# Value products of a head pair moved behind the next pair's transposes, and a context layer that steps by whole heads

## What is computed

```python
# first block, per layer: 3 mixers x 8 heads
s = q @ k.T * scale + bias              # 256 x 256 per head, chunk-causal or causal
p = softmax(s)
y_h = p @ v_h                           # 64 wide per head
branches = stack([y_a, y_b, y_c]); proj = branches @ w_branch
merged = sum(sigmoid(x @ w_gate + b_gate) * proj) @ w_out

# second block, context layer: 8 heads, each with two score maps
p = softmax(q @ k.T / 8)                # q, k: 2 maps x 64 wide
a = p[:, 0] - lam * p[:, 1]
y_h = a @ v_h                           # 128 wide per head
```

## Time and profile before

| | us |
|---|---|
| median of 3 runs | 2656.06 (2655.84 to 2657.03) |
| the profiled execution | 2656.9 |
| its span, first to last instruction | 2655.1 |
| PE busy | 2633.1 (99%) |
| POOL busy | 1941.5 (73%) |
| ACT busy | 1419.6 (53%) |
| DVE busy | 1179.5 (44%) |

### The profile page before, as it was taken

How to read it: one execution, slowest core, us unless ns; L and a number is a source line. 1 busy time by engine, 2 the same in 40 slices (tenths; PEclk the granted TensorE clock), 3 DMA queues, 4 the chain that set the end, 5 groups by cost and what they waited for, 6 DMA issues and landing times.

```text
span 2655.1 us, 44218 instructions
## 1 busy us (share of the span) xinstructions
PE 2633.1 (99%) x17695; PEld 2292.0 (86%) x17695; DVE 1179.5 (44%) x2347; ACT 1419.6 (53%) x2002; POOL 1941.5 (73%) x816
## 2 busy tenths in 40 slices
PE   9999999999999999999999999999999999999999
PEld 8878889989878899888789998887899988878898
DVE  3443342234334433434435553545445544542655
ACT  5755554447565544455654446556544455564543
POOL 6657668856667488687677886866768877668787
PEclk9999999999999999999999999999999999999999
DMA  7556475565565655664454555644445565345453
GB/s 291 204 217 230 157 248 185 188 231 191 212 231 192 230 189 185 198 213 160 156 175 161 189 190 184 204 149 137 158 153 196 185 220 178 129 135 177 165 191 127
DMA packets 139085, 498.43 MB, mean 188 GB/s; under 512 B 15488, under 2 KB 17664, under 8 KB 137984
## 3 DMA queue, kind: packets, MB, share of 16 engines
q1 hardware_dynamic: 132768, 480.52, 53.6%
q10 hardware_dynamic: 6112, 15.08, 1.7%
HBM read 492.39 MB, written 3.15 MB: 187 GB/s over the span
## 4 chain that ended last, share of the span: by engine, by line
PE 94%; DVE 2%; ACT 1%; DVEq 1%; issue 0%; ACTq 0%; DMA 0%; SPq 0%; POOL 0%
PE lin L796 13%; PE lin L614 12%; PE lin L664 11%; PE lin L665 11%; PE lin L668 11%; PE aux L610 5%; PE aux L614 5%; PE aux L611 5%; PE lin L610 5%; PE lin L611 5%; PE aux L1183 2%; PE aux L1201 1%; PE aux L874 1%; PE aux L842 1%; PE lin L842 1%; PE aux L1190 1%
## 5 line engine op out<-in xcount | busy, mean ns | idle before, releaser
L576 POOL TENSOR_TENSOR wlo<-raw,whi 128x1024 fp32r<-128x1024 f32 x812 | 1941.3, 2407 | 703.4 <-ACT whi L1300 695.4
L1300 ACT ACTIVATE whi<-raw 128x1024 fp32r<-128x1024 f32 x811 | 845.3, 1057 | 649.6 <-PE lin L668 259.7
L796 PE MATMUL lin<-in_both,whi 128*128 128x512 f32 x1600 | 401.6, 393 | 0.2
L664 PE MATMUL lin<-whi,in_both 128*128 128x512 f32 x942 | 378.8, 402 | 0.3 <-DVE mods_all L1824 0.3
L665 PE MATMUL lin<-whi,in_both 128*128 128x512 f32 x942 | 368.1, 391 | 0.0
L614 PE MATMUL lin<-in_both,wlo 128*128 128x256 f32 x2560 | 365.7, 283 | 0.1
L614 PEld LDWEIGHTS lin<-in_both,wlo 128*128 128x128 f32 x2560 | 346.1, 192 | 16.1 <-POOL wlo L576 0.5
L796 PEld LDWEIGHTS lin<-in_both,whi 128*128 128x128 f32 x1600 | 287.7, 189 | 53.1 <-DVEq L2287 0.8
L2272 DVE TENSOR_REDUCE Z<-lin 128x512 f32<-128x1024 f32 x100 | 122.4, 1224 | 298.4 <-PE lin L614 297.0
L668 PE MATMUL lin<-wlo,in_both 128*128 128x512 f32 x944 | 253.6, 390 | 0.0
L610 PE MATMUL lin<-in_both,whi 128*128 128x256 f32 x920 | 234.6, 291 | 6.8 <-ACT whi L1762 6.4
(11 more groups left out here) (293 smaller groups left out, 3682.7 us busy)
## 6 DMA issues: line engine op xcount, KB each, us to landing
raw<-in_wstream SPq DMA_DIRECT2D x907, 512.0 KB, 3.5
gate_row<-in_gate_bias ACTq DMA_DIRECT2D x12, 256.0 KB, 3.3
Z<-in_rel ACTq DMA_DIRECT2D x2, 1536.0 KB, 11.5
Z<-in_mem_t ACTq DMA_DIRECT2D x2, 1024.0 KB, 7.2
kv_store<-Z ACTq DMA_DIRECT2D x2, 1024.0 KB, 8.9
Z<-kv_store ACTq DMA_DIRECT2D x2, 1024.0 KB, 9.9
Z<-in_ctx_t SPq DMA_DIRECT2D x1, 1024.0 KB, 7.3
out_x<-x SPq DMA_DIRECT2D x4, 256.0 KB, 2.5
```

The lines of the kernel that those rows point to most:

```text
L576: pool.tensor_tensor(wlo[s][:, :], raw[i % RAWS][:, :], whi[s][:, :].bitcast(F32), ALU.subtract).then_inc(lo_pool, 1)
L664: pe.matmul(out, xh, wh, start=start, stop=False, skip_group_check=True)
L796: pe.matmul(lin[:, p, up * CH:(up + 1) * CH], wh[:, w], in_both[:, :, k * T:(k + 1) * T], start=(k == 0), stop=(k == KD - 1), skip_group_c ...
L1300: act.activation(whi[s % SLOTS][:, :], raw[i % RAWS][:, :], ACT.Copy).then_inc(hi_ready, 1)
```

## The change

**First block.** `pair_values(p - 1)` now stands between `pair_transposes(p)` and `pair_scores(p + 1)`, so the fill of a pair is one stretch; only the last pair keeps its value products between fill. The products are written into columns 384 to 511 of banks 2 and 3 (`pair_output`), which makes six matmuls of 128 columns out of two of 256 and two of 128. The modulation tiles of both heads of a pair add up in bank 0, so DVE adds one row tile per pair instead of two. ACT takes `pair_hi(p - 1)` at the head of the pair and waits for `y_lo_done` before it copies the transposed probabilities; DVE takes `pair_lo(p - 1)` at the head of the pair, before `lowest`. The transposed modulation columns go to bank 1, and PE waits for `mod_added` ahead of the scores of the seventh pair.

**Context layer.** Where `kts == 2`, the 16 half-head steps become 8 head steps (`head_scores`, `head_transposes`, `head_outputs`, `head_exps`, `head_highest`, `head_combine`). The matmuls are the same ones; fill goes in blocks of 3 units before the values and 1 or 2 before the transposes, 36 units as before.

```diff
+HEAD_BEFORE_T = [1, 2] * (NH // 2)
+HEAD_BEFORE_V = [3] * NH
...
+        pair_output = aux[:, 2:4, SW:CH]
+        mod_out = aux[:, 1, SW:SW + 2 * TURN]
...
                 for g in heads:
-                    modulation_tile(aux[:, g % 2, SW:CH], g % TURN, True, True)
+                    modulation_tile(aux[:, 0, SW:CH], g % TURN, g == heads[0], g == heads[1])
+                if p and 2 * p % TURN == 0:
+                    pe.wait_ge(mod_added, t.ahead(mod_added, 2 * p // TURN))
...
+                for tt in range(2):
+                    for e in range(2):
+                        pe.matmul(aux[64 * e:64 * e + 64, 2 + tt, SW:CH], v[:, (h + e) * 64:(h + e + 1) * 64],
+                                  probs_tr(e)[:, tt * P:(tt + 1) * P], start=True, stop=(tt == 0), skip_group_check=True)
                 for e in range(2):
-                    pe.matmul(aux[64 * e:64 * e + 64, 2, 0:T], v[:, (h + e) * 64:(h + e + 1) * 64], probs_tr(e)[:, 0:T],
...
@@ PE, first_layer
                     pair_transposes(p)
+                    if p:
+                        pair_values(p - 1)
                     if p + 1 < PAIRS:
                         pair_scores(p + 1)
                     advance(fill, BEFORE_PV[p])
-                    pair_values(p)
+                    if p + 1 == PAIRS:
+                        pe.wait_ge(pt_ready, t.next(pt_ready, 2))
+                        pair_values(p)
                     advance(fill, AFTER_PV[p])
...
@@ ACT, first_layer
                 for p in range(PAIRS):
+                    if p:
+                        pair_hi(p - 1)
+                        act.wait_ge(y_lo_done, t.next(y_lo_done))
                     for e in range(2):
                         transposed(SW, e)
...
@@ DVE, first_layer
                 for p in range(PAIRS):
+                    if p:
+                        pair_lo(p - 1)
+                    if (2 * p + 2) % TURN == 0:
+                        modulation_bias(l, 2 * p + 2 - TURN, mod_out, TURN).then_inc(mod_added, 1)
...
@@ PE, second_layer
-                for n in range(STEPS):
+                if kts == 2:
+                    for h in range(NH):
+                        advance(fill, HEAD_BEFORE_T[h])
+                        head_transposes(h)
+                        if h + 1 < NH:
+                            head_scores(h + 1)
+                        advance(fill, HEAD_BEFORE_V[h])
+                        head_outputs(h)
```

More of the change, by code:

```diff
@@ L1205, in diff_values, with head_scores, head_transposes, head_outputs @@
                     t.skip(yb_taken)
+            def head_scores(h):
+                for tt in range(2):
+                    for m in range(2):
+                        q = zt(Q2 + h)[64 * m:64 * m + 64, tt * P:(tt + 1) * P]
+                        mm = pe.matmul(aux[:, m, tt * T:(tt + 1) * T], q, head_keys(m, h, 2), start=True, stop=True)
+                mm.then_inc(scores_done, 1)
+            def head_transposes(h):
+                pe.wait_ge(probs_ready, t.next(probs_ready))
+                for i in range(4):
+                    c = h % 2 * CH + i * P
+                    mm = pe.transpose(aux[:, 2, i * P:(i + 1) * P], probs[:, c:c + P], ident)
+                mm.then_inc(trans_done, 1)
+            def head_outputs(h):
+                if t.ahead(yb_taken, 0):
+                    pe.wait_ge(yb_taken, t.ahead(yb_taken, 0))
+                if h == 0:
+                    pe.wait_ge(values_ready, t.next(values_ready))
+                pe.wait_ge(pt_ready, t.next(pt_ready))
+                for tt in range(2):
+                    for kt in range(2):
+                        i = 2 * tt + kt
+                        mm = pe.matmul(aux[:, 3, tt * P:(tt + 1) * P], probs_tr(0)[:, i * P:(i + 1) * P], head_values(h, kt, 2),
+                                       start=(kt == 0), stop=(kt == 1))
+                    mm.then_inc(pv_done, 1)
+                t.skip(yb_taken)
             def second_fill():
@@ L1249, in second_layer @@
                 fill = second_fill()
-                for n in range(STEPS):
+                if kts == 2:
+                    for h in range(NH):
[5 more added lines that the diff above has]
+                        head_outputs(h)
+                for n in range(STEPS if kts == 4 else 0):
                     advance(fill, DIFF_BEFORE_T[n])
@@ L1660, in diff_exps, with head_exps @@
                 act.drain().then_inc(exp_done, 1)
+            def head_exps(h):
+                act.wait_ge(maxed, t.next(maxed))
+                for tt in range(2):
+                    for m in range(2):
+                        s = aux[:, m, tt * T:(tt + 1) * T]
+                        i = slice(2 * tt + m, 2 * tt + m + 1)
+                        act.activation(s, s, ACT.Exp, bias=stat(h, "minus", 4)[:, i], accum_out=stat(h, "total", 4)[:, i])
+                act.drain().then_inc(exp_done, 1)
             def gates_out(p, dst):
@@ L1729, in second_layer @@
                 fill = second_fill()
-                for n in range(STEPS):
+                if kts == 2:
+                    for h in range(NH):
+                        advance(fill, HEAD_BEFORE_T[h])
+                        transposed(CH)
+                        if h + 1 < NH:
+                            head_exps(h + 1)
+                        advance(fill, HEAD_BEFORE_V[h])
+                for n in range(STEPS if kts == 4 else 0):
                     advance(fill, DIFF_BEFORE_T[n])
@@ L1952, in lowest @@
                                              accum_out=stat(g, "minus")[:, tt:tt + 1])
[L1953 to L1956, removed]
+                if g % 2 == 0:
+                    rows, new = mod_rows(g), aux[:, 0, SW:CH]
+                    i = copy(rows, new) if g % TURN == 0 else tt_(rows, rows, new, ALU.add)
+                    if (g + 2) % TURN == 0:
+                        i.then_inc(mod_row, 1)
                 settle().then_inc(maxed, 1)
```

80 lines of the change are left out of this document (61 added, 19 removed).

## The result

The changed kernel takes 2661.62 us (median of 22 runs, 2659.43 to 2663.21), the kernel before 2656.71 in the same comparison (22 runs, 2655.38 to 2659.13). The ratio is 1.0017, with a 95% interval of 1.0011 to 1.0024: 4.9 us slower, within the 0.2% that I had called no change, and 0.6 us above the upper end of my range. The forecast was 2657.0. It stood on a median of three runs, 2656.06; with 22 runs the kernel before is at 2656.71, so the difference was forecast at +1.0 and measured at +4.9.

A forecast was written before the change was run, and what follows sets the result against it. PE, busy 99% of the span, was taken to bound the kernel. First block +4.9 and context layer -3.9 gave +1.0 on the 2656.06 us median: forecast 2657.0, range 2648 to 2661.

The forecast's parts named there:

- The interruption: First block, PE: a value step costing 1.01 us in the fill costs 0.75 to 0.80 behind transposes, 0.24 saved.
- The chain of the second and third pair: First block: ACT and DVE run late, so PE waits some 2.7 us per layer before its fourth feature chunk.
- Rival A: First block: the third pair's delay hides and does not reach PE; 2648.6 us, chance 0.20.
- Rival C: First block: the value step is not cheaper behind transposes, +3.8, 2660.8 us; chance 0.07.
- rival B: The clock falls in the new wait, 1.7 us per layer: 2660.4 us, far end 2663; chance 0.18.
- The sixth pair's wait: First block: PE's scores wait for DVE's `mod_added` behind the forget tiles, 0.8 us per layer.
- The eleventh pair's values: First block: these products still follow the twelfth pair's transposes, where before they were done: +0.75 us per layer.
- The context layer: Whole-head steps save 0.40 us a head, -3.2 for eight, plus -0.7 for two waits: -3.9.
- the old waits: Context layer: PE's two waits, for ACT's copy behind a gate and for DVE, would go, worth -0.7 us.

The follow-up runs named there:

- the busy short wait: The change plus 11 bf16 matmuls of zeros in PE's wait before the fourth feature chunk: 2659.33 us, ratio 1.0007 to the kernel before.
- the long one: The change with ACT's third-pair probability copies done three times and 18 matmuls on zeros in each lengthened wait: 2663.97 us, ratio 1.0022 to the kernel before.
- the first block's part alone: First block as changed, context layer in half-head steps as in the kernel before: 2664.19 us, ratio 1.0028 to the kernel before.
- The longer bare wait: The change with ACT's third-pair probability copies done three times, PE left idle in the wait: 2667.61 us, ratio 1.0037 to the kernel before.
- the new context table: The change with value steps 1, 2, 3, 5 kept in the fill, later forget tiles and another context fill table: 2648.56 us, ratio 0.9967 to the kernel before.

## Why the prediction was wrong

**The interruption, 1.01 to 0.75 or 0.80:** right. It is 0.80, the dear end, and yet an interval is 0.22 to 0.28 shorter, around the 0.24 taken.

**The chain of the second and third pair:** right in each step. ACT goes on at 99.79 (forecast 99.9), PE starts its next feature chunk at 105.68 (105.9), the wait is 2.6 (2.7), PE is 2.6 behind at the fourth pair (2.8). Ahead of it PE waits near 72 and 84, 1.1 and 1.0 from start to start, and the third pair's transposes come at 94.05 instead of 93.55: the forecast's "nothing is gained, everything is 0.5 late". Rival A is out. It is the second pair's value step that bites there: keeping that one step in the fill gives back 2.2 of the 2.6. Rival C is out too, as the value step measured 0.80.

**The step that failed first: the clock behind the wait.** It was rival B, with a chance of 0.18, and I forecast a granted clock of 1.00 from 103 to 112. It is 0.50 in one of the two layers of both profiles of the change, and the sum held nothing for it. The forecast's difference was 3.9 short (+1.0 against +4.9); of that the stretches leave 2.1 to the clock, the busy short wait says 2.3, the long one 2.4, and the first block's part alone only 0.8. What I set against B (dense fill around the pause, and waits of about 1 us that left the clock alone) said nothing about 2.6, as no wait of that length was in the trace; a case that no row speaks against should have had more weight. The price was near: 1.7 each forecast, 1.4 and 1.5 measured, but not in every layer and execution. The Trainium skill (TensorE: Matmul & The Clock Gate, section HAM oscillation) describes a kernel in which waits of about 3 to 5 us between dense bursts put the array back to half its clock each time. The longer bare wait agrees (0.50 behind it in both layers of its profile). The forecast wait of 2.7 is shorter than those, so B did not follow from that page; behind the measured 2.6 the clock fell in two of six profiled waits.

**The wait behind the forget keys, 0.5 a layer, missing from the sum.** I asked of each moved step whom its own results make late, and not what it had covered. ACT's evacuation of 1.02 ran beside the fifth pair's values and the forget keys together; with the values gone the keys' 0.67 are too short. The rows of before near 134 show both side by side.

**The sixth pair's wait:** forecast 0.8, measured 0.7 (0.91 from start to start, where 0.2 is normal). Right.

**The eleventh pair's values:** +0.75 forecast, and from the twelfth pair's transposes to the merged output it is +0.9.

**The context layer, -3.9, or -3.2 if the waits come back:** -3.2. A head step's parts are 0.52 for the transposes and 1.07 for the scores, as forecast:

```profile
1284.38 0.60 PE L1228 MATMUL aux<-c,probs 128*128 128x128 f32 x4
1284.90 1.13 PE L1221 MATMUL aux<-Z 64*128 64x256 f32 x8
1285.97 0.50 PE L667 MATMUL lin<-whi,in_both 128*128 128x512 f32 x1
```

But the same fewer and larger steps that let the old waits go put four times 0.44 of DVE's work in one piece ahead of a tap that PE waits for.

**The sum.** Forecast +1.0. Forget keys +1.0, context layer +0.7, the chain at the fourth pair -0.4, the clock +2.3: +4.6, against a measured +4.9 and +4.5. That the two are so near is in part luck: without the clock these terms give +2.3 and the stretches +2.8, and the clock's 2.3 is the least certain of them. The direction and most terms were right. The range took B without its far end and held no term for a cover that is taken away. How far it was missed says little: on the 2656.06 that the forecast stood on, +4.9 is 2661.0, just at its upper end.

## What to carry to other kernels

When a step leaves a stretch of an engine, look at what ran on the other engines beside it: it was somebody's cover, and what it hid comes out as a wait even if all its own results come in time. Where a chain of ACT and DVE is already without a pause, do not put another link in it; one step left in its old place gave back 6.8 in both layers, clock and all, more than the 4.8 that all the others can save at 0.24 each. A new wait of TensorE in dense work, of 2.6 us or more as here, should be charged with a chance of the clock behind it as well, and a few matmuls on zeros into an unused bank take that part away while the wait itself is being removed.

## What the runs showed of the hardware

A wait of 2.6 us in dense fill left the clock at 1.00 in four profiled cases and brought it to 0.50 (1.2 GHz) for 3.4 us in two; one of 4.85 (start to start, as the 2.6 is) brought it to 0.50 for 6.8 us in both profiled cases. Waits of 0.7 to 1.5 us, start to start, in this fill left it at 1.00 in every profile.

Of all thirteen profiles of this case ten have one or two more stretches of 3.4 us at half clock, at one or two of three places with many small matmuls and a wait of 1.45, start to start (near 360, 560 and 920); the other three have none there. The kernel before has one. Near 360, 560 and 920 such a fall costs 1.3 us (339.5 against 338.2 between the layers, 532.26 against 530.94 in the context part), so a difference between two profiles needs the clock's stretches taken off before it is put down to an edit: without that, 1.3 of the new context table's gain would have been the clock's.
